# RWKV recurrence: the level's product with X taken over both heads of a pair, with Z as two diagonal blocks

## The reference

```
def step(S, inp):
    r_t, w_t, k_t, v_t, a_t, b_t = inp
    sa = einsum('bhij,bhj->bhi', S, a_t)
    S = S * w_t[:, :, None, :] + sa[..., None] * b_t[:, :, None, :] + v_t[..., None] * k_t[:, :, None, :]
    return S, einsum('bhij,bhj->bhi', S, r_t)
```

## Time and profile before

| what | us |
|---|---|
| median of 3 runs | 1716.98 |
| the profiled execution, its own time | 1712.7 |
| its span, first to last instruction | 1710.8 |
| TensorE busy with matmuls | 1467.0 (86%) |
| TensorE busy with weight loads | 896.3 (52%) |
| VectorE busy | 625.1 (37%) |
| ScalarE busy | 362.9 (21%) |
| GpSimd busy | 207.5 (12%) |

### The profile page before, as it was taken

One profiled execution on the slowest core, in us unless ns is written; L12 is line 12 of the kernel. 1 busy time (PEld: TensorE's weight loads), 2 busy tenths in 40 slices (PEclk: granted clock), 3 DMA queues, 4 the chain that ended last, 5 costly groups with the idle time before them and its releaser, 6 DMA issues. The chain is left out here.

```text
span 1710.8 us, 27396 instructions
## 1 busy us (share of the span) xinstructions
PE 1467.0 (86%) x10717; PEld 896.3 (52%) x10718; DVE 625.1 (37%) x1016; ACT 362.9 (21%) x789; POOL 207.5 (12%) x253
## 2 busy tenths in 40 slices
PE   6999999876789985469975999996798399999968
PEld 4666666554678873224432444443587244444423
DVE  1122551188145544813344111111686511111117
ACT  1232110177233322100010111111232011111111
POOL 3000000000333313100001101111300111001030
PEclk8999999977699997779996999998599599999988
DMA  6672120031000000051037788874502797876453
GB/s 183 145 304 80 25 50 0 27 83 26 2 4 4 4 4 8 0 163 38 26 140 272 261 295 273 303 283 140 195 1 101 239 318 241 307 257 229 176 201 133
DMA packets 137059, 236.96 MB, mean 139 GB/s; under 512 B 20178, under 2 KB 100115, under 8 KB 136682
## 3 DMA queue, kind: packets, MB, share of 16 engines
q1 hardware_dynamic: 113458, 151.01, 27.8%
q0 software_dynamic: 16880, 60.41, 9.6%
q10 hardware_dynamic: 6624, 24.12, 3.5%
HBM read 178.84 MB, written 58.21 MB: 139 GB/s over the span
## 5 line engine op out<-in xcount | busy, mean ns | idle before, releaser
L2200 PE MATMUL ex_pb<-ew_w_gate_up,ex_xT 128*128 x736 | 329.5, 601 | 6.0 <-DVE ex_xT L2245 2.3
L298 PE MATMUL pj_pb<-pj_xT,pj_w 128*128 128x348 f32 (+3 forms) x960 | 282.1, 455 | 0.5 <-ACT pj_xT L322 0.5
L298 PEld LDWEIGHTS pj_pb<-pj_xT,pj_w 128*128 128x128 f32 (+1 forms) x960 | 179.0, 187 | 101.4 <-issue 0.6
L2200 PEld LDWEIGHTS ex_pb<-ew_w_gate_up,ex_xT 128*128 128x128 f32 x736 | 137.9, 192 | 164.8 <-issue 164.0
L2183 PE MATMUL ex_pb<-ew_w_down,ex_hiddenT 128*128 x368 | 165.8, 593 | 3.4 <-ACT ex_hiddenT L2270 3.4
L2393 DVE TENSOR_TENSOR ex_hidden<-ex_hidden,ex_pb 128x256 f32<-128x256 f32 x46 | 19.4, 421 | 324.2 <-ACT ex_hidden L2265 324.2
L2183 PEld LDWEIGHTS ex_pb<-ew_w_down,ex_hiddenT 128*128 128x128 f32 x368 | 66.4, 191 | 69.8 <-issue 69.8
L1932 PE MATMUL mo_pb<-mo_w,minus_kk_then_y 128*128 128x512 f32 (+1 forms) x144 | 65.6, 608 | 21.7 <-DMA mo_w<-in_w_out 21.7
L2388 DVE COPY ex_y_rows<-ex_pb 128x512 f32<-128x512 f32 x46 | 31.8, 691 | 134.5 <-PE ex_pb L2183 134.5
L430 DVE SCALAR_TENSOR_TENSOR mixed<-pj_pb,v_mu,mixed 128x347 f32<-128x347 f32 (+3 forms) x42 | 24.0, 572 | 145.7 <-ACT mixed L372 145.6
L1932 PE MATMUL mo_pb<-mo_w,projected_qkv 128*128 128x512 f32 (+1 forms) x144 | 66.4, 616 | 8.6 <-DMA mo_w<-in_w_out 8.6
(11 more groups left out here) (414 smaller groups left out, 2057.6 us busy)
## 6 DMA issues: line engine op xcount, KB each, us to landing
ew_w_gate_up<-in_w_ex_gate SPq DMA_DIRECT2D x32, 1024.0 KB, 7.8
ew_w_gate_up<-in_w_ex_up SPq DMA_DIRECT2D x32, 1024.0 KB, 10.7
ew_w_down<-in_w_ex_down SPq DMA_DIRECT2D x32, 1024.0 KB, 12.8
scratch_slots_out<-ex_y_rows ACTq DMA_DIRECT2D x46, 512.0 KB, 5.1
scratch_slots_out<-pj_tmp POOLq DMA_DIRECT2D x4, 4096.0 KB, 16.5
scratch_x_stored<-x_rows SPq DMA_DIRECT2D x16, 512.0 KB
pj_w<-in_w_in SPq DMA_DIRECT2D x7, 1024.0 KB, 8.5
minus_kk_then_y<-in_x_prompt SPq DMA_DIRECT2D x8, 512.0 KB, 5.4
```

Of the source, the lines that this page charges most:

```text
L298: last = nc.tensor.matmul(product(at)[:, 0:tn], w[:, s % NW, k, c0:c0 + mrows], xT[:, k, x0:x0 + tn], start=(k == 0), stop=(k == KD - 1))
L2200: last = mm(pb[:, 2 + u, :], xT[:, u, k, :], w[:, k, :], start=(k == 0), stop=(k == KD - 1))
```

## The change

`Z` gets an extra axis of two, so that for a pair and a chunk it is 128 partitions by 64 columns. `take_z` writes all of it: it reads the 32 columns of the product twice and multiplies with a mask that is the level's mask on the diagonal (head 0 to the first 32 columns, head 1 to the last 32) and zero beside it. `level_x` then takes all 128 rows of X and of Z in one product for a pair and chunk, 8 products of 128 x 64 weights with 64 moving columns, and writes them side by side into columns 256 to 511 of bank 6. `take_x` adds them with one instruction over all 8 heads. The masks in DRAM and SBUF are twice as wide.

```diff
-        Z = m.sb("Z", [P, 2, 4, HALF])
+        Z = m.sb("Z", [P, 2, 4, 2, HALF])
...
                 for t in range(4):
-                    for par in range(2):
-                        for ch in range(2):
-                            last = mm(pb[fr(ch), 6 + par, P * t:P * t + HALF], X[fr(par), ch, t, :], Z[fr(par), ch, t, :],
-                                      start=True, stop=True)
+                    for ch in range(2):
+                        last = mm(pb[fr(ch), 6, 256 + CH * t:256 + CH * t + CH], X[:, ch, t, :],
+                                  Z[:, ch, t, :, :].rearrange("p a b -> p (a b)"), start=True, stop=True)
                 last.then_inc(q["x"], 1)
...
             def take_z(n, lev):
                 dve.wait_ge(q["z"], NLEV * n + lev + 1)
-                tt(flat(Z[:, :, :, :]), columns(6, 0, HALF), eight(f"lev{lev + 1}T"), ALU.mult).then_inc(q["zc"], 1)
+                both = columns(6, 0, HALF).unsqueeze(2).to_broadcast([P, 8, 2, HALF])
+                of_head = const[f"lev{lev + 1}T"][:, :].rearrange("p (a b) -> p a b", a=2)
+                tt(Z[:, :, :, :, :].rearrange("p c t a b -> p (c t) a b"), both,
+                   of_head.unsqueeze(1).to_broadcast([P, 8, 2, HALF]), ALU.mult).then_inc(q["zc"], 1)
 
             def take_x(n, lev):
                 dve.wait_ge(q["x"], NLEV * n + lev + 1)
-                for par in range(2):
-                    new = halves_of(XT[:, n % 2, :, par, :], lev, 1)
-                    out = pb[:, 6 + par, :].rearrange("p (t s) -> p t s", t=4)[:, :, 0:HALF]
-                    last = tt(new, new, out.rearrange("p t (g b) -> p t g b", b=2 << lev), ALU.add)
-                last.then_inc(q["xe"], 1)
+                new = halves_of(XT[:, n % 2, :, :, :].rearrange("p t a s -> p (t a) s"), lev, 1)
+                out = pb[:, 6, 256:512].rearrange("p (h g b) -> p h g b", h=HA, b=2 << lev)
+                tt(new, new, out, ALU.add).then_inc(q["xe"], 1)
...
+    tabs.update({k: np.kron(np.eye(2), chunk[k]) for k in LEVELS})
...
-            mix_const.update({k: sb(layer0, f"k_{k}", [P, CH // 2]) for k in LEVELS})
+            mix_const.update({k: sb(layer0, f"k_{k}", [P, CH]) for k in LEVELS})
```

## The result

The changed kernel takes 1704.07 us (median of 20 runs, 1693.65 to 1714.16) against 1715.97 us for the kernel before (median of 20 runs, 1708.33 to 1725.91).

What follows compares the result with a forecast made beforehand. TensorE was taken to bound the recurrence, half of it fixed time of tiny instructions. Seams +7.9 us and fewer issue waits -0.9 gave +7.0 on 1714.8, so 1722 us; range 1710 to 1733.

Steps and rivals of the forecast that it cites:

- seams: TensorE's switches between matmul forms around each level's product, with the longer block: +0.99 us a pass, +7.9 in eight.
- pauses: TensorE's waits named "issue" in the recurrence: 11% fewer instructions take 11% off 7.6 us, -0.9 us.
- The overlap of two blocks in one form: Levels 1 and 4: product starts within the preceding 128*64 block's loads; without it, 0.15 us more at each.
- Z covered: VectorE's Z takes 0.26 us longer in each of 40 levels, hidden behind TensorE's other work.
- constants free: Five DMAs of GpSimd's queue carry 32 KB instead of 16, over 400 us before use: 0.
- Seams hidden, stalls fewer: Rival in the recurrence: seams halved from 7.9, issue waits down 7.6 us, about 1711 us; chance 0.13.
- The chance for over 1% faster: TensorE would have to save 0.43 us in every level, nearly all of the product's 0.47; chance 0.02.

Runs made afterwards that it cites:

- e4: Kernel before with only the change's wide Z (masks twice as wide); product on quarters and two additions kept: 1715.94 us, ratio 1.0014 to the kernel before.
- e1: Kernel before, level product untouched, pairs of 64x64 products in b_k_by_a and b_k_by_r merged into one with 128 weight columns: 1718.96 us, ratio 1.0021.
- e3: The change applied only at levels 1 and 4, the other levels as in the kernel before: 1709.77 us, ratio 0.9975 to the kernel before.
- e5: Changed kernel with level_z issued twice at each level, 64 more loads and matmuls a level: 1733.06 us, ratio 1.0115 to the kernel before.
- e6: Changed kernel with level_x issued twice at each level, 32 more loads and matmuls a level: 1725.77 us, ratio 1.0060 to the kernel before.
- e8: Kernel before with the 8 slow transposes of end_rows issued five times: 1735.72 us, ratio 1.0117 to the kernel before.
- e9: Changed kernel with TensorE's order at level 3 rewritten for fewer seams and level 2's product back on quarters: 1703.37 us, ratio 0.9925 to the kernel before.
- e2: Changed kernel with products merged in b_k_by_a and b_k_by_r too: 1719.39 us, ratio 1.0026 to the kernel before.

## Why the prediction was wrong

The forecast had two terms, +7.9 for seams and -0.9 for pauses. The first was nearly right, the second is the step that failed.

**The seams: right.** level_z starts each level, so its starts cut a pass. Before, with one pause of 0.50 in the fifth level and one of 0.15 in the fourth (level 2 starts at 536.36):

```profile
528.60 0.56 PEld L1178 LDWEIGHTS rc_pb<-rc_XT,rc_L 64*64 64x64 f32 x32 [0.17 <-issue]
...
531.86 0.60 PEld L1178 LDWEIGHTS rc_pb<-rc_XT,rc_L 64*64 64x64 f32 x32
...
540.14 0.19 PEld L1178 LDWEIGHTS rc_pb<-rc_XT,rc_L 64*64 64x64 f32 x4
...
544.64 0.20 PEld L1178 LDWEIGHTS rc_pb<-rc_XT,rc_L 64*64 64x64 f32 x7
545.34 0.48 PEld L1178 LDWEIGHTS rc_pb<-rc_XT,rc_L 64*64 64x64 f32 x25 [0.50 <-issue]
...
549.44 0.56 PEld L1178 LDWEIGHTS rc_pb<-rc_XT,rc_L 64*64 64x64 f32 x32 [0.17 <-issue]
```

After:

```profile
500.70 0.56 PEld L1178 LDWEIGHTS rc_pb<-rc_XT,rc_L 64*64 64x64 f32 x32 [0.17 <-issue]
...
502.76 0.55 PEld L1187 LDWEIGHTS rc_pb<-rc_Z,rc_X 128*64 128x64 f32 x16
503.38 1.02 PEld L1140 LDWEIGHTS rc_pb<-decay_sums,rc_b_k_scaled 64*64 64x64 f32 x64
504.31 0.56 PEld L1178 LDWEIGHTS rc_pb<-rc_XT,rc_L 64*64 64x64 f32 x32
...
506.97 0.19 PEld L1187 LDWEIGHTS rc_pb<-rc_Z,rc_X 128*64 128x64 f32 x2
507.07 0.25 PEld L1209 LDWEIGHTS rc_pb<-k_ident,mixed 128*64 128x64 f32 x2
...
508.54 0.56 PEld L1178 LDWEIGHTS rc_pb<-rc_XT,rc_L 64*64 64x64 f32 x32
...
512.86 0.19 PEld L1178 LDWEIGHTS rc_pb<-rc_XT,rc_L 64*64 64x64 f32 x4
...
517.48 0.56 PEld L1178 LDWEIGHTS rc_pb<-rc_XT,rc_L 64*64 64x64 f32 x32
...
521.65 0.56 PEld L1178 LDWEIGHTS rc_pb<-rc_XT,rc_L 64*64 64x64 f32 x32 [0.17 <-issue]
```

| level | before, us | after, us | measured | forecast |
|---|---|---|---|---|
| 0 | 3.26 | 3.61 | +0.35 | +0.35 |
| 1 | 4.50 | 4.23 | -0.27 | -0.13 |
| 2 | 3.78 | 4.32 | +0.54 | +0.45 |
| 3 | 4.50 - 0.15 | 4.62 | +0.27 | +0.32 |
| 4 | 4.80 - 0.50 | 4.17 | -0.13 | 0 |

+0.76 us a pass instead of +0.99, 6.1 us in 8 passes. The block takes 0.62 us to the next one (502.76 to 503.38). The overlap of two blocks in one form, on which I had to choose, exists: at level 1 the product's first loads (506.97) lie among L1209's last (507.07). Those starts and the seams agree with the rule that the Trainium skill gives in TensorEngine Tiling (Array Packing), section Key Properties, for a drain at a change of mode.

**Z covered, constants free: right.** e4 and the waits for Z show it; e4 also has the wider constants.

**The pauses: wrong by a factor of 14.** The step read: "If they come with the number of instructions, 11% is -0.9 us." It was wrong twice. The base was too small: 7.6 us from two groups of matmuls, where the long pauses before the weight loads were 13 us, and the lower clock behind them added 2 to 3 us more, in passes of 25.3 and 25.0 us instead of 20.2; this is what is left of the passes when their pauses are taken off. And the law was wrong: the pauses don't fall in proportion to the number but go with the rate. From 72.5 to 62.4 per us, 14% less, all but 0.8 us of them went. Balance of the recurrence: 6.1 us for seams, 13.1 - 0.8 = 12.3 us of pauses and 2 to 3 us of low clock gone, 8.2 to 9.2 gained, of 9.9 measured. How much of the low clock the pauses themselves brought is not shown.

**The rivals.** "Seams hidden, stalls fewer" (1711 us, chance 0.13) named the right lever, but said that the seams would hide, which they don't, and also took 7.6 us as all there was. With the seams at the forecast's whole 7.9, and 13 us and the low clock in place of the 7.6, it would have come to 1707. The chance for over 1% faster rested on the claim that TensorE must save 0.43 us in every level; TensorE's idle time between blocks could give as much.

**What is shown and what is argued.** That the pauses go with the rate of instructions, wherever they stand, is shown by e1, e3, e5, e6, e8 and e9. That they are a wait for instructions to arrive is seen in the transfers of the DMA queue named "instruction", in 458 to 645 us, before and after (packets, MB, share):

```profile
q8 instruction: 46, 0.75, 1.6%
```

```profile
q8 instruction: 41, 0.67, 1.5%
```

46 packets for 11,478 loads and matmuls and 41 for 10,259 are 250 for each, 16 KB each. The pauses keep to these packets in two ways. They stand one or more whole packets apart, and each ends at the same distance behind the start of a packet. Two pauses of the kernel before that are neighbours, with 126 loads between them:

```profile
496.65 0.42 PEld L1178 LDWEIGHTS rc_pb<-rc_XT,rc_L 64*64 64x64 f32 x18 [0.65 <-issue]
...
500.36 0.89 PEld L1252 LDWEIGHTS rc_pb<-decay_sums,rc_ST 64*64 64x64 f32 x28 [1.25 <-issue]
```

and the packet of the pause that ends at 486.22, in the window 483.75 to 484.00; up to 487.50 no other begins:

```profile
q8 instruction: 1, 0.02, 25.3%
```

The share of 25.3% of 16 engines in 0.25 us is 1.0 us for the packet. The same for all pauses of 0.5 us and more between 480 and 630 us, the packets' starts read in windows of 0.1 us:

| pause ends, us | length, us | packet began before, us | loads since the pause above |
|---|---|---|---|
| 486.22 | 1.50 | 2.5 | |
| 496.65 | 0.65 | 2.4 | 253 = 2 x 126 |
| 500.36 | 1.25 | 2.4 | 126 |
| 511.81 | 0.86 | 2.5 | 378 = 3 x 126 |
| 523.54 | 1.00 | 2.4 | 380 = 3 x 127 |
| 545.34 | 0.50 | 2.4 | 757 = 6 x 126 |
| 567.35 | 1.06 | 2.9 | 757 = 6 x 126 |
| 586.11 | 0.53 | 2.4 | 631 = 5 x 126 |
| 597.70 | 1.50 | 2.6 | 382 = 3 x 127 |
| 611.53 | 1.52 | 2.6 | 379 = 3 x 126 |
| 623.27 | 1.21 | 2.6 | 377 = 3 x 126 |

(A wait of 0.52 us that ends at 604.09 is left out: it is the short one of 0.23 us before the transposes of level 2, at the lower clock.) The next packet began 1.0 to 1.4 us after each of these pauses. The pauses of 0.6 us and more in e3, e4, e5, e6, e8 and e9 do the same: they end 2.2 to 2.9 us behind the start of a packet. So this queue carries TensorE's program while it runs, and a pause is TensorE at the end of one packet with the next not yet there. A limit can be estimated from this: 1.2 us from a pause's end to the start of the next packet and 2.5 us from there to the next pause's end are 3.7 us for 252 loads and matmuls, 68 per us. The neighbours 496.65 and 500.36 are 3.71 us apart. A packet whose work is denser leaves a pause for the rest of the 3.7 us; with 64 of these instructions in 0.47 us the densest could leave 1.8 to 1.9 us by this estimate, and the longest pause in these runs is 1.78 (e4). This also says why pauses begin at a mean of 63, below the limit: a single packet can be denser than its pass. No experiment changed the transfer itself.

## What to carry to other kernels

When an engine shows waits named "issue" of a us or more in the middle of a block, add them all up, note the granted clock behind them, and compute instructions per us for that stretch. Then look whether the pauses stand whole packets of the instruction queue apart. Near the rate at which they set in, replacing many small instructions by fewer of the same total time can be worth the whole sum, not its share. Once they are gone, fewer instructions give nothing more (e2: the pass grew by just what its slower blocks cost), and seams between forms are what counts. Look at the waits as well as the time: e1 won and lost the same 14 us.

## What the runs showed of the hardware that I had not expected

- TensorE ran out of instructions at about 63 to 73 weight loads and matmuls per us, with pauses of up to 1.8 us (e4) at the ends of packets of about 250. Behind two of the three pauses of 1.5 us in the kernel before, the granted clock fell to the lower level (a mean of 0.75 over 6 to 7 us); behind the third, and behind those of e3 and e5, it did not.
- In the form 64*128 with float32 and 64 moving columns, 32 loads and matmuls took 1.86 us (e1), 60 ns a pair; the same work as 64 pairs on quarters took 1.02 us.
- In the form 128*64, two blocks of products follow without a gap, but a block of products followed by transposes in that form keeps 0.06 us.
